# A two-block model step in float32: score levels one projection later, and the recurrence's gates as plain four-byte products

## The reference

```python
def hgrn2_mixer(h, w_in, lb, norm_w, w_out):      # cut
    ...                                            # q = silu, f = lb + (1 - lb) sigmoid, k = 1 - f
        rel = bb[:, :, :, None, :] - bb[:, :, None, :, :]
        decay = jnp.exp(jnp.where(causal, rel, -jnp.inf))
        scores = jnp.einsum('bhtk,bhtsk,bhsk->bhts', qb, decay, kb)
        o = jnp.einsum('bhts,bhsv->bhtv', scores, vb) + ...
def rglru_mixer(h, w_in, conv_w, conv_b, wa, ba, wx, bx, lam, w_out):
    y, u = jnp.split(h @ w_in, [LRU_WIDTH], axis=-1)
    y = jax.nn.gelu(y)
    uc = conv_b + sum of 4 taps of u
    r = jax.nn.sigmoid(jnp.einsum('bsnc,ncd->bsnd', ub, wa) + ba)    # ub: uc in 4 blocks of 256
    ig = jax.nn.sigmoid(jnp.einsum('bsnc,ncd->bsnd', ub, wx) + bx)
    log_a = -LRU_C * r * jax.nn.softplus(-lam)
    a = jnp.exp(log_a)
    b_in = jnp.sqrt(-jnp.expm1(2.0 * log_a)) * (ig * uc)
    hs = scan of (a, b_in) over the tokens
    return (hs * y) @ w_out
```

## Time and profile before

| | |
|---|---|
| median of 3 runs | 1166.98 us (1166.65 to 1169.16) |
| the profiled execution | 1169.06 us, span 1167.8 us |
| TensorE busy | 1133.4 us, 97% of the span |
| DVE, ACT, POOL busy | 668.0, 581.5, 294.7 us |
| mean granted TensorE clock | 0.99 of full speed |
| bytes moved by DMA | 207.48 MB, mean 178 GB/s |

### The profile page before, as it was taken

How to read it: one execution, slowest core, us unless ns; L and a number is a source line. 1 busy time by engine, 2 the same in 40 slices (tenths; PEclk the granted TensorE clock), 3 DMA queues, 4 the chain that set the end, 5 groups by cost and what they waited for, 6 DMA issues and landing times.

```text
span 1167.8 us, 19379 instructions
## 1 busy us (share of the span) xinstructions
PE 1133.4 (97%) x8149; PEld 1052.4 (90%) x8149; DVE 668.0 (57%) x1042; ACT 581.5 (50%) x889; POOL 294.7 (25%) x193
## 2 busy tenths in 40 slices
PE   7999999999999999998999999999999869999997
PEld 6999989999889999888998889999889859999986
DVE  6655756667656454258697555433257786533424
ACT  6645555556445544347433545444434945444432
POOL 2022100000015444504121115444400001544440
PEclk9999999999999999999899999999999989999999
DMA  8679574554547665655443447655655434666560
GB/s 262 224 229 312 162 238 124 169 176 140 175 146 214 198 186 193 199 156 179 136 145 108 142 149 225 189 181 187 209 163 170 156 112 143 214 186 194 186 193 36
DMA packets 155152, 207.48 MB, mean 178 GB/s; under 512 B 9471, under 2 KB 128409, under 8 KB 155066
## 3 DMA queue, kind: packets, MB, share of 16 engines
q1 hardware_dynamic: 151274, 193.11, 52.9%
q0 software_dynamic: 3792, 13.15, 3.4%
HBM read 205.01 MB, written 4.24 MB: 179 GB/s over the span
## 4 chain that ended last, share of the span: by engine, by line
PE 88%; DVE 6%; ACT 3%; issue 1%; DMA 1%; POOL 0%; SPq 0%; DVEq 0%; ACTq 0%; POOLq 0%
PE bank L496 18%; PE bank L499 18%; PE bank L502 18%; PE bank L519 9%; PE bank L516 9%; PE bank L513 9%; DVE wlo L1363 2%; PE bank L852 2%; ACT whi L953 1%; PE bank L778 1%; PE bank L788 1%; DMA area<-in_hgrn_lb 1%; PE bank L800 1%; PE bank L559 1%; DVE uc L1493 0%
## 5 line engine op out<-in xcount | busy, mean ns | idle before, releaser
L1363 DVE TENSOR_TENSOR wlo<-raw,whi 128x1024 fp32r<-128x1024 f32 x279 | 343.4, 1259 | 230.3 <-ACT whi L953 229.3
L953 ACT ACTIVATE whi<-raw 128x1024 fp32r<-128x1024 f32 x366 | 364.4, 1044 | 114.3 <-PE bank L519 109.4
L496 PE MATMUL bank<-hh,whi 128*128 128x256 f32 x1784 | 287.0, 282 | 1.7 <-ACT hh L985 1.7
L1938 POOL TENSOR_TENSOR wlo<-raw,whi 128x1024 fp32r<-128x1024 f32 x87 | 223.4, 2568 | 255.9 <-ACT whi L953 255.9
L499 PE MATMUL bank<-hh,wlo 128*128 128x256 f32 x1784 | 282.3, 280 | 0.0
L502 PE MATMUL bank<-hl,whi 128*128 128x256 f32 x1784 | 282.0, 279 | 0.0
L496 PEld LDWEIGHTS bank<-hh,whi 128*128 128x128 f32 x1784 | 242.5, 188 | 6.7 <-issue 5.5
L499 PEld LDWEIGHTS bank<-hh,wlo 128*128 128x128 f32 x1784 | 241.6, 188 | 0.0
L502 PEld LDWEIGHTS bank<-hl,whi 128*128 128x128 f32 x1784 | 241.2, 188 | 0.0
L1945 POOL TENSOR_TENSOR st<-st,half 128x1 f32<-128x1 f32 x18 | 10.3, 582 | 354.6 <-DVE st L1380 325.8
L513 PE MATMUL bank<-whi,gh 128*128 128x512 f32 x264 | 81.5, 390 | 0.0
(11 more groups left out here) (314 smaller groups left out, 1262.4 us busy)
## 6 DMA issues: line engine op xcount, KB each, us to landing
raw<-in_ffn_w_in SPq DMA_DIRECT2D x88, 512.0 KB, 3.6
raw<-in_w_in SPq DMA_DIRECT2D x72, 512.0 KB, 5.0
raw<-in_ffn_w_out SPq DMA_DIRECT2D x44, 512.0 KB, 3.3
raw<-in_hgrn_w_in SPq DMA_DIRECT2D x32, 512.0 KB, 4.4
raw<-in_w_ffn_gate SPq DMA_DIRECT2D x22, 512.0 KB, 4.5
raw<-in_w_ffn_up SPq DMA_DIRECT2D x22, 512.0 KB, 4.2
raw<-in_w_ffn_down SPq DMA_DIRECT2D x22, 512.0 KB, 3.3
raw<-in_w_branch SPq DMA_DIRECT2D x16, 512.0 KB, 4.5
```

The source lines that it names most:

```text
L496: T.matmul(out, wh[:, i, c], xh[:, k, :], start=first and (i, k) == pairs[0], stop=False)
L953: A.activation(half_of(whi, j, h), half_of(raw, j, h), ACT.Copy).then_inc(s_hi[j % NS][h], 1)
L1363: V.tensor_tensor(half_of(wlo, j, h), half_of(raw, j, h), half_of(whi, j, h).bitcast(f32), ALU.subtract).then_inc(s_lo[j % NS][h], 1)
L1938: G.tensor_tensor(half_of(wlo, j, 1), half_of(raw, j, 1), half_of(whi, j, 1).bitcast(f32), ALU.subtract).then_inc(s_lo[j % NS][1], 1)
```

## The change

Behind `hq` j the level list now goes only over the pairs below j. All levels of a pair thus come one projection later, and the last list (`rest`) is one for both groups. `outputs(0)` moves to behind the first part of `hv` of group 1. The first half of `outputs` no longer waits for level 8.

The two `lg` units are gone. Their weights are loaded unsplit into a buffer `gw` of their own, by eight transfers that SP issues between the loads of the feed-forward before the recurrence. Each gate product is one plain float32 product of `gw` and `uc` in place of three. `conv_round` and `conv_rest` are gone. Both `lru_gates` stand ahead of `ly` 0, and ACT's and DVE's steps are reordered around them.

```diff
@@ build: buffers and the list of weight units
+        gw = sbuf(lr, "gw", [128, 2, 4, 512])
         lr.close()
...
-        def lru_gate_unit(h):
-            blocks = slice(2 * h, 2 * h + 2)
-            unit(("lg", h), [(256 * i, 256, a[name][0, blocks].rearrange("b (c p) n -> p (b c) n", p=128))
-                             for i, name in enumerate(("lru_wx_2", "lru_wa_2"))], 4, 512)
-
         for j in range(4):
             cols(("lu", j), lw, 1024 + 256 * j, 256)
-        lru_gate_unit(0)
         cols(("ly", 0), lw, 0, 256)
-        lru_gate_unit(1)
         cols(("ly", 1), lw, 256, 256)
...
         for j in range(1, 4):
             advance(("hf", j), range(j))
-            advance(("hq", j), range(j + 1))
+            advance(("hq", j), range(j))
         for g2 in range(2):
             for name in ("hv", "hg"):
                 for part in range(2):
                     advance((name, g2, part), range(4))
-            while min(at_level[2 * g2:2 * g2 + 2]) < 9:
-                advance(("rest", g2), range(4))
+                    assert (name, g2, part) != ("hv", 1, 0) or min(at_level[0:2]) == 9
+        while min(at_level) < 9:
+            advance(("rest",), range(4))
@@ tensor_program
                     for j in (2 * g2, 2 * g2 + 1):
                         tq.wait_ge(*evac("lev", j, 7))
-                        tq.wait_ge(*evac("lev", j, 8))
+                        if tt == 1:
+                            tq.wait_ge(*evac("lev", j, 8))
...
-                    b = turn(("tr", 4, c), c % 2)
+                    b = turn(("tr", 4, c), 6 + c if c < 2 else c - 2)
...
+            def behind(name, g2, part):
+                levels(name, g2, part)
+                if (name, g2, part) == ("hv", 1, 0):
+                    outputs(0)
+
             for g2 in range(2):
                 for name in ("hv", "hg"):
-                    project_tokens((name, g2), 3, lambda part: levels(name, g2, part))
-                if g2 == 0:
-                    levels("rest", 0)
-                    outputs(0)
+                    project_tokens((name, g2), 3, lambda part: behind(name, g2, part))
             turn_outputs((0, 1))
-            levels("rest", 1)
+            levels("rest")
             outputs(1)
...
             def lru_gates(h):
-                u = unit_at["lg", h]
-                wh, wl = whole(whi, u), whole(wlo, u)
+                tq.wait_ge(s_gw, 128)
                 for i in range(2):
                     for n in (2 * h, 2 * h + 1):
                         b = turn(("lg", i, n), next_bank())
-                        for z in range(2):
-                            tq.wait_ge(*hi_set(u, z))
-                            tq.wait_ge(*lo_set(u, z))
-                        tq.wait_ge(s_ucl, n + 1)
+                        tq.wait_ge(s_conv, 8 + 2 * n + 2)
                         tq.wait_ge(*free(("lg", i, n)))
...
-                                T.matmul(out, wh[:, k - 4 * h, c], ch[:, k, :], start=k == 2 * n, stop=False)
-                                T.matmul(out, wh[:, k - 4 * h, c], cl[:, k, :], start=False, stop=False)
-                                tok = T.matmul(out, wl[:, k - 4 * h, c], ch[:, k, :], start=False, stop=k == 2 * n + 1)
+                                tok = T.matmul(out, gw[:, h, k - 4 * h, c], uc[:, k, :], start=k == 2 * n, stop=k == 2 * n + 1)
...
             project_columns(("lu", 3), 6)
             lru_gates(0)
+            lru_gates(1)
             project_columns(("ly", 0), 6)
-            lru_gates(1)
             project_columns(("ly", 1), 6)
@@ scalar_program (the recurrence; outputs and levels are moved as on TensorE)
-            conv_round(0)
             conv_start(2)
-            conv_round(1)
             use(("lu", 3))
             conv_start(3)
-            conv_round(2)
-            use(("lg", 0))
             lru_gates(0)
-            conv_round(3)
             use(("ly", 0))
             tangents(0)
-            use(("lg", 1))
             lru_gates(1)
             tangents(1)
-            use(("ly", 1))
             decays(0)
             decays(1)
+            use(("ly", 1))
             for n in range(4):
                 root_of(n)
             use(("ly", 2))
             gelu(0)
             gelu(1)
             gated(0)
-            gelu(2)
             gated(1)
             use(("ly", 3))
+            gelu(2)
+            gated(2)
             gelu(3)
-            gated(2)
             gated(3)
@@ vector_program (the recurrence)
-            conv_rest(0)
-            u_of(2)
-            conv_rest(1)
-            use(("lu", 3))
             conv_unit(2)
             u_of(3)
-            conv_rest(2)
-            use(("lg", 0))
             conv_unit(3)
-            conv_rest(3)
-            use(("ly", 0))
+            use(("lu", 3))
             gated_input(0)
             gated_input(1)
-            y_of(0)
-            use(("lg", 1))
-            use(("ly", 1))
+            use(("ly", 0))
             gated_input(2)
             gated_input(3)
             input_factor(0)
             input_factor(1)
-            y_of(1)
+            y_of(0)
             input_factor(2)
             input_factor(3)
+            use(("ly", 1))
             scan(0)
             scan(1)
+            y_of(1)
             use(("ly", 2))
-            y_of(2)
             gated(0)
             scan(2)
             gated(1)
+            scan(3)
             use(("ly", 3))
-            scan(3)
+            y_of(2)
+            gated(2)
             y_of(3)
-            gated(2)
             gated(3)
@@ sync_program
             for j in range(NS, NU):
                 load(j, 0)
                 load(j, 1)
+
+                k = j - unit_at["g", 1, 2]
+                if 0 <= k < 8 and k % 2 == 0:
+                    h, c = k // 4, k // 2 % 2
+                    for i, name in enumerate(("lru_wx_2", "lru_wa_2")):
+                        src = a[name][0, 2 * h + c].rearrange("(c p) n -> p c n", p=128)
+                        S.dma_start(gw[:, h, 2 * c:2 * c + 2, 256 * i:256 * i + 256], src).then_inc(s_gw, 16)
```

More of the change, by code:

```diff
@@ L346, in build @@
         s_osq, s_og = sem("o_squared"), sem("og_set")
-        s_pad, s_uch, s_ucl = sem("pad_set"), sem("ch_set"), sem("cl_set")
+        s_pad, s_uch, s_gw = sem("pad_set"), sem("ch_set"), sem("gate_weights_landed")
         s_ax, s_aa, s_ti, s_tr, s_root, s_scan = (sem(n) for n in ("input_gate_set", "decay_set", "gated_input_set", "factor_set", "root_set", "scanned"))
@@ L920, in lru_gates @@
                             for k in (2 * n, 2 * n + 1):
-                                T.matmul(out, wh[:, k - 4 * h, c], ch[:, k, :], start=k == 2 * n, stop=False)
-                                T.matmul(out, wh[:, k - 4 * h, c], cl[:, k, :], start=False, stop=False)
-                                tok = T.matmul(out, wl[:, k - 4 * h, c], ch[:, k, :], start=False, stop=k == 2 * n + 1)
+                                tok = T.matmul(out, gw[:, h, k - 4 * h, c], uc[:, k, :], start=k == 2 * n, stop=k == 2 * n + 1)
                         tok.then_inc(s_full[b], 1)
-                used[u, 0] = used[u, 1] = full("lg", 1, 2 * h + 1)
             project_pair([("lu", 0), ("lu", 1)], 6)
@@ L1272, in conv_start @@
                     conv_first(uc[:, c, :], up, c, 40, 72, evac("col", "lu", j), s_conv0)
[L1274 to L1277, removed]
             def lru_gates(h):
@@ L1310, in gated @@
                 aq.wait_ge(s_gy, n + 1)
-                aq.wait_ge(*used[unit_at["lg", 1], 1])
                 A.activation(ch[:, sl, :], yg[:, sl, :], ACT.Copy).then_inc(s_uch, 1)
@@ L1846, in conv_unit @@
                     conv_taps(uc[:, c, :], up, c, 40, 8 + c + 1)
-            def conv_rest(j):
-                sl = slice(2 * j, 2 * j + 2)
-                vq.wait_ge(s_uch, j + 1)
-                V.tensor_tensor(cl[:, sl, :], uc[:, sl, :], ch[:, sl, :].bitcast(f32), ALU.subtract).then_inc(s_ucl, 1)
             def gated_input(n):
@@ L1877, in gated @@
                 V.tensor_tensor(yg[:, sl, :], yg[:, sl, :], ig[:, sl, :], ALU.mult).then_inc(s_gy, 1)
-                vq.wait_ge(s_uch, 4 + n + 1)
+                vq.wait_ge(s_uch, n + 1)
                 V.tensor_tensor(cl[:, sl, :], yg[:, sl, :], ch[:, sl, :].bitcast(f32), ALU.subtract).then_inc(s_hs, 1)
@@ L1883, in vector_program @@
             use(("lu", 2))
+            u_of(2)
             conv_unit(1)
-            conv_rest(0)
-            u_of(2)
-            conv_rest(1)
-            use(("lu", 3))
             conv_unit(2)
             u_of(3)
-            conv_rest(2)
-            use(("lg", 0))
             conv_unit(3)
-            conv_rest(3)
-            use(("ly", 0))
+            use(("lu", 3))
             gated_input(0)
             gated_input(1)
-            y_of(0)
-            use(("lg", 1))
-            use(("ly", 1))
+            use(("ly", 0))
             gated_input(2)
```

## The result

Four runs of the changed kernel took 1152.85 to 1154.97 us, median 1154.3; four of the kernel before, with them, 1166.65 to 1169.83, median 1168.07. The ratio is 0.989 (95% interval 0.9874 to 0.9906), a gain of 11.0 to 14.7 us. The profiled execution took 1154.97 us with a span of 1153.7, against 1169.06 and 1167.8 before: 14.1 us less, where 15.0 were forecast. The forecast for the median was 1152.0; of the 2.3 us between it and 1154.3, 1.1 are the median of before, which was 1166.98 in the runs that it was made from.

A forecast was written before the change was run, and what follows sets the result against it. TensorE, busy 1133.4 us, was taken to set the time. Second mixer 6.5 plus recurrence 8.5, loads nothing, made 15.0 us: 1169.06 to 1154.1 for the profile, 1152.0 us for the median, range 1149 to 1160.

The forecast's parts named there:

- Second mixer: Levels one projection back: 3.4 us of wait, 2.65 of low clock and 0.4 at pair 2, sum 6.5 us won.
- What is late next? ... I take no loss: Second mixer: three levels move behind token projections, adding 3.9 us of DVE work; no loss taken, 3.9 us as bound.
- The 2.65 us for the clock: Second mixer: one level and one unit behind the silu wait take 9.25 us, losing 2.65 us to the clock.
- Recurrence: DVE's stretch from 888.2 to 956.6 shrinks from 68.4 to 59.6 us; walking both queues gives 8.5 us, taken.
- the stall at the third unit: Recurrence, output product `lo`: TensorE waits about 4.6 us for ACT's copy of the third unit, 3.3 before.
- the second unit's stall: Recurrence, output product `lo`: TensorE waits 1.3 us for the second unit's `wlo`.
- the edit adds 2.7 us to the engine that sets the time: Recurrence gates on TensorE: 32 plain products, 14.1 us, replace 96 split products, 11.4 us.
- The 4.2 us counted for the gates: Recurrence on TensorE: 6.9 us of losses go, less 2.7 of added products, so `ly` 3 ends 4.2 us earlier.
- the tail of the recurrence does not follow: Rival: only TensorE's 4.2 us are won in the recurrence, the other 4.3 are lost; 1156.3 us, chance 0.13.
- The loads: Eight 256 KB transfers pulled ahead into the second block's first feed-forward; no cost taken.
- the feed-forward starves: Rival: pulled-ahead loads starve the feed-forward, 21.6 us lost if all exposed, 1173.6 us; chance 0.04.
- Nothing moves: Rival: what is won at a wait is lost at the next one, about 1166 us; chance 0.04.

The follow-up runs named there:

- the mixer alone: Kernel before with only the second mixer's level lists, last list and moved outputs; recurrence as before: 1163.28 us, ratio 0.9963.
- this part alone: Changed kernel with the second mixer put back as before, so only the recurrence's edits: 1159.6 us, ratio 0.9926.
- more halves on POOL: Changed kernel with later POOL multiplication and earlier third-unit copy, plus POOL sharing DVE's rests of five recurrence units: 1156.7 us median, ratio 0.9902.

## Why the prediction was right, point by point

**Second mixer, 6.5 us predicted, 5.5 measured.** The mechanism was right: level 0 of pair 1 no longer waits for `qT`, and the clock from 551 to 562 is 1.00, as was to be seen. The step "What is late next? ... I take no loss" failed, by 1.0 us, and it accounts for the difference: with the wait for `kT` removed the mixer gains 6.77 us. The prediction looked for DVE's load, and between 592 and 617, where it looked, TensorE never waited. The wait lies at 651, and DVE had been idle for 2.8 us ahead of the stretched step. I followed DVE's queue alone and not what POOL does at the same moment, and took 1.30 us for every level from two rows that meet no POOL instruction. The Trainium skill has the rule that was needed ("SBUF — State Buffer", section Who interferes with whom): a DVE instruction with both inputs in SBUF and a GpSimd instruction that reads SBUF contend for a shared read interface, and the sharing is an exclusive lock. The trace agrees, to 0.15 us: DVE's step begins 0.12 us behind POOL's and takes 1.42 us, where it would be 1.27 - 0.12 + 0.42 = 1.57 with DVE blocked to the end of POOL's row; without POOL it takes 0.43.

**The 2.65 us for the clock** was one execution's figure. The same place gave 1.6 us in another kernel behind the same wait (8.18 - 6.60). A slow stretch is a cost with a spread of about 1 us. That is also why the mixer alone gives 5.5 us by its stretch and 4.3 by the ratio of its runs. The eleven runs of the kernel before spread wider still, from 1163.8 to 1171.0 us, and no run shows why. The sum took its prices from an execution that was 2.1 us above the median, and carried them over to the median whole.

**Recurrence, 8.5 us predicted, 8.5 measured** (9.2 with this part alone). The gates came as forecast, one block of 13.63 us up to the next start (891.75 to 905.38), against 14.1 by the row. The estimate worked out from the Trainium skill's four passes ("FP8 and Floating Point Precision", section TensorE Precision Notes), 0.427 us each, gives 13.7: so the page's was the better price, and the sum by the one row 0.4 us too high. DVE's stretch was forecast as 49.1 us of work and 10.5 of idle time, together 59.6; measured are 49.0 and 10.8, together 59.8. DVE's wait for the first decays is 4.6 (4.8 forecast), the stall at the third unit 4.6 (4.6), and its copy is 8.7 us earlier against the start of the part (8.5): 14.25 less the 5.58 by which the part starts earlier. Only the second unit's stall was put too long, 0.8 us (0.15 and 0.64) and not 1.3.

**A step that was right in its sum and misleading in its reason**: "the edit adds 2.7 us to the engine that sets the time". In this part TensorE does not set it. Up to about 10 us of extra products ahead of `lo` cost nothing; the end is set by the queue of ACT and DVE and, at its end, by the place of one copy. The 4.2 us counted for the gates were never added to the sum, which came from walking ACT's and DVE's queues, and that saved the forecast. The rival "the tail of the recurrence does not follow" rested on the same picture and is out.

**Where the 8.5 us come from**: removed work 6.15, order 2.4. The order is one edit: with ACT and DVE in the new order and the second gates at their old place the recurrence takes 98.76 us, 2.3 more than with the old order throughout. ACT there waits 5.1 us, in four pieces, for the products of the later gates. Each figure here is from one execution or two.

**The loads** cost nothing, as taken: TensorE is busy for all of the 50 us from 690 to 740, and ACT waits for a weight transfer for 0.4 us in the whole run (0.6 before). That the feed-forward starves is out, and so is "Nothing moves".

**What was left on the table**: the forecast named the stall of 4.6 us at the third unit and did not ask whether it was needed. One moved copy takes it away, for 4.1 us.

## What to carry to other kernels

An engine that is 97% busy over the span need not be the bound in the part that is edited: price an edit by the queue whose end the next part waits for, and put a few dummy products on the busy engine, at the place in question, to see what it has to spare there. When steps are moved, look at what the neighbours do at the same moment: a 0.4 us step on the path became one of 1.4 us, since it met a POOL instruction. And once a forecast names a wait that will be left, look at once whether the one step it waits for can stand earlier; that was worth a third of the whole change.

## What the runs showed of the hardware

- Float32 instructions of DVE with two tensor inputs were stretched by a large POOL product of two tensors that was running, by about what POOL still had to do: 0.42 to 1.42 us in the kernel after, 0.69 to 2.90 and 2.84, 0.48 to 2.46, and 1.22 to 3.36 with more halves on POOL. The kernel before has it too, 0.41 to 1.49 in the mixer and 1.22 to 3.42 in the feed-forward (at 704.94). So POOL's 2.5 us for half a rest can cost DVE's chain more than the 1.2 us that DVE takes for it itself.
- POOL waits as well: in the kernel after its five small products for `tot` take 1.66 us at 543.09, where DVE is idle, and 4.01 at 551.38, where DVE sets two rests one after the other (2.36 us from 551.37).
- The granted clock falls not only behind one long wait: it was 0.59 (over 4.1 us) behind four waits of 0.34 to 1.11 us (TensorE busy for 4.40 of the 6.80 us ahead, still at 1.00), 0.57 behind one of 4.64 us, and 1.00 throughout where extra products filled the gap.
- The slow stretch behind the same 3.1 us wait cost 2.65 us in one execution, 2.8 in a second (9.38 - 6.60) and 1.6 in a third.
